# Another order of pieces and another map of the on-chip memory ahead of the first expert window

## The chip, the cores and the metric

The kernel runs on one core of one Trainium2 chip. The metric is the device time of one execution in microseconds (us); lower is better.

## What is computed

One inference step of a two-layer decoder trunk, all in fp32, for 512 prompt tokens and 8 new sample tokens (width 1024). Layer 0 mixes tokens with differential attention (8 heads; the sample tokens read a paged cache of keys and values), layer 1 with a short convolution. Each layer then runs PEER, a lookup of experts:

```
h = LN1(alpha*h + mixer(h))
h = LN2(alpha*h + PEER(h))
h = h + sigmoid(h @ Wg) * (p_i @ Wp)

PEER, per token: q = h @ w_q; scores of 8 heads against 2 x 128 keys; top 16 of each half,
top 16 of the 256 sums -> 16 expert ids and softmax gates g per head (128 experts a token)
a = <h, u_tab[id]>;  out = sum over experts of g * gelu(a) * v_tab[id]
```

Every token needs 128 rows of u and v (4 KB each) out of two tables of 16384 rows in each layer. The outputs are the rows h, the new keys and values of layer 0, and the convolution's state.

## The kernel before

**The engines' queues.** The program is written by hand for each engine. A planner (`Plan`) makes one list of "pieces" and every engine walks that list in its order and does its own part of each piece, so an engine that waits in one piece holds up all pieces behind it on that engine. TensorE makes products into four PSUM banks in turn, ScalarE (ACT) or VectorE (DVE) empties each bank, SyncE (SP) loads 1 MB panels of weights into two panel buffers, and GpSimd (POOL) issues the gathers of experts and the loads of cache pages.

**The lead.** First come 16 products of queries and keys. Then the list `lead` holds the attention: 32 units of scores (`score`), softmax on DVE and ACT (`weigh`), transposes (`turned`), and after each second unit of a head the sum over values (`summed`). Between them lie products that fill TensorE: value rows (`values[p][b]`, panel p and token tile b), key rows to be stored (`key_rows`), and the sample tokens' attention: `s_new`, `s_turn`, `s_probs`, `p_turn`, and the eight `s_out` products `out[k][half]`, each of which needs two samples' value pages. There is room for two samples' pages at a time, so POOL loads the next two when `out[k][1]` has read the last ones. `o_turn` transposes four samples' results. `square`, `ms0`/`ms1`, `root`, `factors` and `rms0`/`rms1` are the per-head normalization of the attention's output; group 0 is tiles 0 and 1, group 1 is tiles 2, 3 and the samples.

At the end of the lead the output projection is made for tile 0 (`m0`, four products, one for each panel of `mix`) and for tile 1 (`m1`), tile 0 is normalized (`a0`, `c0`) and transposed (`t0`), its query features are made (`q`) and its experts are chosen. Each head's choice is four pieces `r[4*hd:4*hd+4]`: key scores on TensorE, then some 10 us of DVE work; the fourth writes the ids that the gathers read, and the gates need an Exp on ACT. Line 1072 does that Exp in piece `route` with `x.i == 3`.

**The expert windows.** A window is one token tile: 128 experts in 64 pairs. For each expert POOL gathers 128 rows of 8 KB (1 MB, line 912) into one of 11 slots of the big on-chip buffer `arena`; DVE forms the dot product (line 1500), ACT the gelu and a diagonal matrix (line 1088), TensorE adds the rows into `acc` (line 1683), and that frees the slot. Background pieces (the next tiles' projections, features and choices) lie between the pairs: `early`, `rest`, `bg` in window 0. DVE and ACT run them two pairs late (`BEHIND = 2`), TensorE at their own place.

**The arena.** During the lead the same `arena` holds the attention's data, so a slot is free for its first gather only when these are dead. Before: slots 0 to 2 hold constants, logits and turned weights; slots 3 to 5 value rows and group 0's attention output; slots 6 to 8 the samples' values and the pages; slots 9 and 10 group 1's attention output, sample rows and factors. Gathers 0 to 5 wait for the ids alone, 6 to 8 for `out[3][1]` (line 909), 9 and 10 for the last `rms1` (line 911):

```
                    if e >= SLOTS_UV:
                        pool.wait_ge(slot_done, e - SLOTS_UV + 1)
                    elif e == HELD_BY_PAGES:
                        pool.wait_ge(bank_full, plan.sample_out[3][1].n + 1)
                    elif e == HELD_BY_SAMPLE:
                        read(pool, plan.last_rms)
```

**SP's queue.** `load_panel` goes through the panels in the order in which they were planned, and waits for the product that last read the buffer. The buffers take turns, but the first `pq` panel has a place of its own in `qT` ("queries"), which waits until all 16 `summed` are done. Ahead of the first `mix` panel (`keys_after`) SP waits for the last value product and loads the PEER keys, since `keys` holds the tokens of group 0 until then.

Of the kernel before, what the change touches and what calls it, by code (L numbers as in the profile page):

```python
# [57 lines left out]
HELD_BY_PAGES = 6  # L58
HELD_BY_SAMPLE = 9
# [60 lines left out]
class Plan:  # L120
# [31 lines left out]
    def settle(self):  # L152

        once = {("pq", 0, 0): "queries"}
# [23 lines left out]
    def lead(self):  # L178
# [4 lines left out]
        key_rows = [[product("k_rows", b=b, half=half) for half in range(2)] for b in range(BLOCKS)]  # L183
        values = [[product("v", self.v_panels[p], p=p, b=b) for b in range(BLOCKS)] for p in range(4)]
        values[0][0].fence = True
# [18 lines left out]
        for b in range(TB):  # L204
            if b >= 2:
                fill[b - 1].append(values[0][b])
            for half in range(2):
                fill[2 * b + half].append(key_rows[b][half])
# [7 lines left out]
        for k in range(4):  # L216
            fill[24 + k + 2 * (k // 2)].append(out[k // 2][k % 2])
        for k in range(2):
            fill[24 + k] += square[2 * k:2 * k + 2]

        lead = values[0][0:2] + key_rows[TB] + [Piece("s_new")]
# [139 lines left out]
    def build(self):  # L361
# [18 lines left out]
        def cut_at(pieces, share):  # L380
# [13 lines left out]
        self.keys_after = m0[0].panel  # L394
# [7 lines left out]
        self.last_rms = rms1[-1]  # L402
# [4 lines left out]
        lead += score[31] + [weigh[30], turned[29], ms0, roots[0], turned[30], f0, weigh[31], summed[6, 1]] + rms0[0] \  # L407
            + [turned[31], m0[0], summed[7, 1], m0[1], f1] + rms0[1] + [m1[0], o_turn[0], out[2][0], m1[1], out[2][1]] \
            + [m0[2], m0[3], a0, m1[2], m1[3], c0] + t0 + q[0:2] + r[0:1] + q[2:4] + r[1:3] + out[3] + [o_turn[1]] + r[3:7] \
            + [ms1, roots[1], f2] + rms1  # L410
        steps = [("alone", 0, 0, [lead])]
        early = r[7:8] + [a1, c1] + t1 + q[4:6] + late[0:2] + r[8:12] + late[2:4]
# [128 lines left out]
def build(nc, h0, h0T, consts, panels, ple_rows, keysT, uv0, uv1, cache_k, cache_v, pages, wlam, subg, ln, convw,  # L541
# [3 lines left out]
    with ctx:  # L545
# [61 lines left out]
        v_flat = part(TB * D)  # L607
        oT_early = part(C * G_W[0]).rearrange("p (c t) -> p c t", c=C)
        assert at[0] <= HELD_BY_PAGES * 2 * D
        at[0] = HELD_BY_PAGES * 2 * D  # L610

        v_new = part(D)
        kv_flat = part(4 * D)
        assert at[0] <= HELD_BY_SAMPLE * 2 * D
        at[0] = HELD_BY_SAMPLE * 2 * D

        oT_late = part(C * G_W[1])
        s_rows = part(D)
        rstd8 = part(G_W[0] + G_W[1])[0:HEADS, :]
        v_rows = [v_flat[:, b * D:(b + 1) * D] for b in range(TB)] + [v_new]  # L620
        oT = [oT_early, oT_late.rearrange("p (c t) -> p c t", c=C)]
        oT_normed = [oT[0], qT[:, q_off[1]:q_off[1] + C * G_W[1]].rearrange("p (c t) -> p c t", c=C)]
        kv_pages = kv_flat.rearrange("p (i j n) -> p i j n", i=2, j=2)


        q_all = oT_late[:, 0:2 * D].rearrange("p (i n) -> p i n", i=2)
# [7 lines left out]
        homes = {0: panel[:, 0, :], 1: panel[:, 1, :], "queries": qT[:, q_free:q_free + 2 * D]}  # L634
# [156 lines left out]
        def _(sp):  # L791
            sp.dma_start(h0T_early, h0T[:, :, 0:G_W[0]]).then_inc(s_hT, 16)

            def load_panel(i):
# [4 lines left out]
                elif home == "queries":  # L799
                    sp.wait_ge(a_o, len(SUMS))  # L800
                sp.dma_start(panel_of(i), panels[PANEL_AT[plan.panels[i]]]).then_inc(s_panel[home], 16)
# [58 lines left out]
        def _(pool):  # L860
# [34 lines left out]
            for b in range(BLOCKS):  # L895
                read(pool, plan.value_rows[b])
                dst = nv_p[b * P:(b + 1) * P, :] if b < TB else nv_s
                pool.dma_start(dst, v_rows[b][0:rows(b), :]).then_inc(v_out, 16)
# [960 lines left out]
```

## Time and profile before

| what | value |
|---|---|
| three runs | 3319.8, 3324.96, 3320.39 us (median 3320.39) |
| the profiled execution | 3319.8 us, of which 3317.9 us from its first to its last instruction |
| mean granted TensorE clock | 0.966 of full speed |
| TensorE, VectorE, ScalarE, GpSimd busy | 91%, 68%, 38%, 37% of the span |
| moved by DMA | 1248.09 MB, 376 GB/s over the span |

In the timeline each row is one or more like instructions: start and duration in us, engine, line, operation, result and operands, and in brackets the idle time of that engine just before and what ended it. PEld is TensorE's weight load. The windows give the busy time of each engine in a stretch, then the granted clock of TensorE (1.00 is 2.4 GHz, 0.50 is 1.2 GHz), the DMA engines' share and what they moved in GB/s.

### The profile page before, as it was taken

The page shows a single profiled execution, that of the slowest core. Times are in us where ns is not written, and L with a number is a line of the kernel's source. Part 1 is how long each engine was busy: PE and PEld are TensorE (multiplying, and loading weights), DVE is VectorE, ACT ScalarE, POOL GpSimd, SP SyncE. Part 2 cuts the span into 40 slices and gives each one's busy share as a digit, 9 for nine tenths or more (in the row PEclk, how much of TensorE's full clock was granted, in tenths as well). Part 3 has the DMA queues.
Part 4 walks back from the last instruction along what each step waited for, and adds up shares of the span by engine and source line. Part 5 has one row for each costly group of instructions (what it writes and reads, how often), then busy time and mean ns, then how long its engine had stood idle before and what let it go on. Part 6 is the DMA issues. An engine that isn't in the chain of part 4 may idle for free.

```text
span 3317.9 us, 33637 instructions
## 1 busy us (share of the span) xinstructions
PE 3011.4 (91%) x9426; PEld 1674.2 (50%) x9426; DVE 2251.0 (68%) x5801; ACT 1268.4 (38%) x3602; POOL 1232.5 (37%) x1100
## 2 busy tenths in 40 slices
PE   8998899989977899998898799999999788888887
PEld 7765555545533456554453355665455344443334
DVE  0653658787467867778768757764667888787454
ACT  0143334344233543333433464332434445435332
POOL 0100233443334333433443334444634435444441
PEclk9999799999999999999999899999999989999999
DMA  4513799999999999999899999999999999999997
GB/s 177 210 73 135 280 386 421 400 414 404 420 421 421 396 413 421 421 421 421 333 421 421 397 372 397 414 418 395 421 421 420 419 380 382 422 402 421 421 422 292
DMA packets 179818, 1248.09 MB, mean 376 GB/s; under 512 B 20086, under 2 KB 23414, under 8 KB 32432
## 3 DMA queue, kind: packets, MB, share of 16 engines
q0 software_dynamic: 156896, 1115.93, 82.3%
q1 hardware_dynamic: 22592, 128.97, 9.8%
q8 instruction: 75, 1.23, 0.1%
q10 hardware_dynamic: 144, 1.05, 0.1%
q14 instruction: 111, 0.91, 0.1%
HBM read 1239.41 MB, written 6.50 MB: 376 GB/s over the span
## 4 chain that ended last, share of the span: by engine, by line
PE 55%; DMA 18%; DVE 16%; ACT 4%; DVEq 4%; issue 3%; ACTq 1%; POOL 1%; POOLq 0%; SPq 0%
PE acc L1683 29%; DMA arena<-in_uv,idx 17%; PE bank L1709 10%; PE bank L1700 7%; DVE arena L1500 7%; PE bank L1538 3%; PE bank L1581 2%; DVEq L1408 2%; ACT diag L1088 1%; ACT L1072 1%; DVE ya L1343 1%; DVE ya L1354 1%; DVE h L1300 1%; DVE yb L1344 1%; DMA arena<-in_uv,small 1%
## 5 line engine op out<-in xcount | busy, mean ns | idle before, releaser
L1683 PE MATMUL acc<-arena,diag 128*128 128x512 f32 x4160 | 1940.1, 615 | 233.5 <-ACT diag L1088 233.1
L912 POOL DMA_INDIRECT arena<-in_uv,idx x1024 | 1185.3, 1158 | 1703.9 <-PE acc L1683 1594.9
L1500 DVE CUSTOM_DVE_ANT_0 arena<-arena,h 128x1024 f32<-128x1024 f32 x1024 | 1217.8, 1221 | 359.9 <-DMA arena<-in_uv,idx 356.8
L1683 PEld LDWEIGHTS acc<-arena,diag 128*128 128x128 f32 x4160 | 795.3, 196 | 1202.5 <-issue 833.2
L1078 ACT ACTIVATE act_w<-dots 128x2 f32<-128x2 f32 x520 | 105.5, 203 | 1433.3 <-DVE dots L1500 1432.7
L1088 ACT ACTIVATE diag<-cst,act_w 128x128 f32<-128x128 f32 x1040 | 368.6, 395 | 122.7 <-PE acc L1683 88.1
L1709 PE MATMUL bank<-hT,panel 128*128 128x264 f32 (+2 forms) x1792 | 403.7, 379 | 3.8 <-ACT hT L1045 3.8
L1709 PEld LDWEIGHTS bank<-hT,panel 128*128 128x128 f32 x1792 | 335.5, 190 | 99.4 <-issue 54.8
L1081 ACT ACTIVATE act_w<-act_w 128x1 f32<-128x1 f32 x1040 | 250.4, 287 | 43.7 <-issue 1.4
L1078 ACT ACT_TABLE_LOAD x128 | 164.2, 1283 | 1.6
L1700 PE MATMUL bank<-panel,hT 128*128 128x256 f32 (+1 forms) x576 | 131.8, 383 | 5.4 <-ACT hT L1045 5.4
L1700 PEld LDWEIGHTS bank<-panel,hT 128*128 128x128 f32 (+1 forms) x576 | 96.9, 170 | 49.3 <-issue 24.4
L1700 PE MATMUL bank<-panel,qT 128*128 128x256 f32 (+1 forms) x512 | 115.9, 379 | 0.0
L1700 PEld LDWEIGHTS bank<-panel,qT 128*128 128x128 f32 (+1 forms) x512 | 83.7, 165 | 40.1 <-issue 17.3
L1072 ACT ACT_TABLE_LOAD x80 | 102.6, 1283 | 1.4
L1337 DVE COPY yb<-tp 128x256 f32<-128x256 f32 x80 | 34.0, 425 | 94.8 <-PE tp L1667 89.6
L1415 DVE SCALAR_TENSOR_TENSOR h<-h,bank 128x256 f32<-128x256 f32 (+1 forms) x40 | 16.7, 419 | 109.0 <-PE bank L1700 107.8
L1500 DVE DVE_READ_ACCUMULATOR2_ANT dots<- 128x1 f32 x1040 | 85.0, 82 | 0.0
L1399 DVE RECIPROCAL ya<-ya 128x1 f32<-128x1 f32 x80 | 13.0, 163 | 83.2 <-ACT ya L1072 83.2
L1538 PE MATMUL bank<-keys,panel 128*128 128x256 f32 x256 | 60.8, 392 | 9.3 <-DMA panel<-in_panels 9.3
L1667 PEld LDWEIGHTS tp<-keys,qT 128*128 128x128 f32 (+1 forms) x320 | 43.3, 172 | 43.1 <-issue 42.1
L1382 DVE TENSOR_TENSOR yb<-ya,cst 128x512 f32<-128x512 f32 x80 | 55.4, 692 | 11.6 <-issue 0.6
(201 smaller groups left out, 2176.1 us busy)
## 6 DMA issues: line engine op xcount, KB each, us to landing
panel<-in_panels SPq DMA_DIRECT2D x103, 1024.0 KB
arena<-in_uv,idx POOLq DMA_INDIRECT x1024
arena<-in_cache_k POOLq DMA_DIRECT2D x16, 512.0 KB, 5.5
arena<-in_cache_v POOLq DMA_DIRECT2D x16, 512.0 KB, 5.0
arena<-out_y_s POOLq DMA_DIRECT2D x8, 512.0 KB, 6.0
arena<-in_panels SPq DMA_DIRECT2D x4, 1024.0 KB, 8.1
lng<-in_ln SPq DMA_DIRECT2D x6, 512.0 KB
lnb<-in_ln SPq DMA_DIRECT2D x6, 512.0 KB
```

The lines of the kernel that those rows point to most:

```text
L912: nc.gpsimd.indirect_dma_start(uv[:, e % SLOTS_UV, :], None, uv_dram[layer], bass.IndirectOffsetOnAxis(ids[:, r:r + 1], 0)).then_inc(gathe ...
L1072: nc.scalar.activation(r_ex, r_tv, ACT.Exp, bias=r_nm, accum_out=r_sum).then_inc(gexp_done, 1)
L1078: nc.scalar.activation(act_w[:, 1, half, s], dots[:, half, s], ACT.Gelu).then_inc(gelu_done, 1)
L1081: nc.scalar.activation(act_w[:, 2, half, r:r + 1], act_w[:, 1, half, r:r + 1], ACT.Copy, scale=act_w[:, 0, half, r:r + 1])
L1088: nc.scalar.activation(diag[:, r % DIAGS, :], mask, ACT.Copy, scale=act_w[:, 2, half, r:r + 1]).then_inc(diag_ready, 1)
L1408: dve.drain()
L1500: V.tensor_tensor_reduce(uv[:, e % SLOTS_UV, 0:D], uv[:, e % SLOTS_UV, 0:D], x_rows, 1.0, 0.0, ALU.mult, ALU.add, dots[:, G % 2, r:r + 1]) ...
L1538: m = mm(pj[n % 2][:, PW + G_OFF[g]:PW + G_OFF[g] + G_W[g]], w[:, c, :], src[g][:, c, 0:G_W[g]], start=(c == 0), stop=(c == C - 1))
L1581: t = mm(product_of[0:m, 0:PW], src[group_of(x.b)][:, c, local(x.b):local(x.b) + m], w[:, c, :], start=(c == 0), stop=(c == C - 1))
L1683: m = mm(acc[:, half * 512:(half + 1) * 512], diag[:, r % DIAGS, :], uv[:, e % SLOTS_UV, D + half * 512:D + (half + 1) * 512], start=False ...
L1700: last = mm(bank[0:m, x.n % BANKS, 0:PW], src[:, c, local(x.b):local(x.b) + m], weights[:, c, :], start=(c == 0), stop=(c == chunks - 1))
L1709: last = mm(bank[:, x.n % BANKS, 0:width], w[:, c, :], hT[:, c, lo:lo + width], start=(c == 0), stop=(c == C - 1))
```

## The change

The arena is mapped anew, pieces of the lead change places, and two of the `mix` panels get a buffer of their own.

- The arena: slots 3 and 4 hold group 1's attention output, sample rows and factors; slots 5 to 10 hold all value rows (the samples' too), group 0's output and the pages. The copies of the sample queries (`q_all`) move to the logits' place. Gathers 0 to 2 wait for the ids alone, 3 and 4 for the last `rms1`, and 5 to 10 for `last_mix`, tile 1's last projection product.
- Panels 2 and 3 of the first `mix` are loaded over the value rows, after all 16 sums are made and all value rows are stored; the PEER keys are loaded ahead of panel 2 instead of panel 0.
- Attention: the value products of tiles 0 and 1 move from the front of the lead into the first two units; the fence for the front goes to the key rows. The four `out` products go from units 24, 25, 28 and 29 to units 25 to 28, and the `square` pieces from 24 and 25 to 28 and 29.
- The end of the lead has a new order: `ms0` ahead of the last scores, tile 1's projection after its first product at the very end, `q[2:4]` and `o_turn[1]` behind the first head's whole choice, `out[3]` ahead of `q[0:2]` in part. The pieces `r[4:7]` go from the lead to the window. A Sqrt of one number ahead of the last squares goes.

```
@@
 FREE_AT_FIRST = 3
-HELD_BY_PAGES = 6
-HELD_BY_SAMPLE = 9
+FREE_NEXT = 5
@@ settle
-        once = {("pq", 0, 0): "queries"}
+        once = {("mix", 0, 2): "values0", ("mix", 0, 3): "values1", ("pq", 0, 0): "queries"}
@@ lead
+        key_rows[TB][0].fence = True
-        values[0][0].fence = True
         for b in range(TB):
-            if b >= 2:
-                fill[b - 1].append(values[0][b])
+            fill[b].append(values[0][b])
...
-            fill[24 + k + 2 * (k // 2)].append(out[k // 2][k % 2])
+            fill[25 + k].append(out[k // 2][k % 2])
-            fill[24 + k] += square[2 * k:2 * k + 2]
+            fill[28 + k] += square[2 * k:2 * k + 2]
-        lead = values[0][0:2] + key_rows[TB] + [Piece("s_new")]
+        lead = key_rows[TB] + [Piece("s_new")]
@@ build
-        self.keys_after = m0[0].panel
+        self.keys_after = m0[2].panel
-        lead += score[31] + [weigh[30], turned[29], ms0, roots[0], turned[30], f0, weigh[31], summed[6, 1]] + rms0[0] \
-            + [turned[31], m0[0], summed[7, 1], m0[1], f1] + rms0[1] + [m1[0], o_turn[0], out[2][0], m1[1], out[2][1]] \
-            + [m0[2], m0[3], a0, m1[2], m1[3], c0] + t0 + q[0:2] + r[0:1] + q[2:4] + r[1:3] + out[3] + [o_turn[1]] + r[3:7] \
-            + [ms1, roots[1], f2] + rms1
+        lead += [ms0] + score[31] + [weigh[30], turned[29], roots[0], f0, turned[30], weigh[31], summed[6, 1]] + rms0[0] \
+            + [turned[31], m0[0], summed[7, 1], m0[1], o_turn[0], out[2][0], m0[2], m0[3], f1, a0] \
+            + rms0[1] + [out[2][1], c0, m1[0]] + t0 + [out[3][0]] + q[0:2] + r[0:4] + [out[3][1], o_turn[1]] + q[2:4] \
+            + [ms1, roots[1], f2] + rms1 + m1[1:4]
-        early = r[7:8] + [a1, c1] + t1 + q[4:6] + late[0:2] + r[8:12] + late[2:4]
+        early = r[4:8] + [a1, c1] + t1 + q[4:6] + late[0:2] + r[8:12] + late[2:4]
@@ load_panel
-                elif home == "queries":
+                elif home in ("values0", "values1", "queries"):
                     sp.wait_ge(a_o, len(SUMS))
+                    sp.wait_ge(v_out, 16 * BLOCKS)
@@ gather_group
-                    elif e == HELD_BY_PAGES:
-                        pool.wait_ge(bank_full, plan.sample_out[3][1].n + 1)
-                    elif e == HELD_BY_SAMPLE:
+                    elif e == FREE_AT_FIRST:
                         read(pool, plan.last_rms)
+                    elif e == FREE_NEXT:
+                        pool.wait_ge(bank_full, plan.last_mix.n + 1)
@@ scalar, lead, ms0
-                    nc.scalar.activation(small[:, 61:62], eps, ACT.Sqrt)
```

## Rows read from the trace of the kernel before

**Rows 1.** The page: busy time, the gathers' queue, the gathers' group.

```profile
PE 3011.4 (91%) x9426; PEld 1674.2 (50%) x9426; DVE 2251.0 (68%) x5801; ACT 1268.4 (38%) x3602; POOL 1232.5 (37%) x1100
...
q0 software_dynamic: 156896, 1115.93, 82.3%
...
L912 POOL DMA_INDIRECT arena<-in_uv,idx x1024 | 1185.3, 1158 | 1703.9 <-PE acc L1683 1594.9
```

**Rows 2.** Windows: lead, first 56 us of the experts, and behind.

```profile
0.00:384.00 384.00, 348.88 (x1609) 255.37 (x1610) 163.20 (x474) 94.63 (x259) 38.76 (x67) 0.94 0.44 162
384.00:440.00 56.00, 50.58 (x182) 28.85 (x180) 37.95 (x88) 22.86 (x66) 24.77 (x20) 0.94 0.90 335
440.00:880.00 440.00, 418.93 (x1274) 231.99 (x1275) 319.44 (x831) 171.93 (x514) 179.03 (x159) 0.97 1.00 411
880.00:1400.00 520.00, 466.37 (x1357) 251.68 (x1356) 380.61 (x990) 206.46 (x597) 207.98 (x190) 0.98 1.01 416
```

**Rows 3.** Timeline where the attention begins.

```profile
127.24 7.14 PE L1581 MATMUL bank<-panel,keys 128*128 128x256 f32 x32 [0.89 <-ACT qT L956]
...
134.86 1.28 DVE L1254 COPY x_sample<-bank 8x512 f32<-8x512 f32 x2 [1.70 <-PE bank L1573]
...
139.89 0.70 PE L1586 MATMUL bank<-qT 64*128 64x256 f32 x2 [3.00 <-DVE small L1220]
```

**Rows 4.** Timeline: the second and third sample products and the pages between.

```profile
252.36 1.91 PE L1629 MATMUL bank<-arena,x_sample 128*32 128x512 f32 x8
...
255.57 0.55 POOL L875 DMA_DIRECT2D arena<-in_cache_v  x1 [10.21 <-issue]
...
264.43 3.44 PE L1629 MATMUL bank<-arena,x_sample 128*32 128x512 f32 x8 [2.13 <-DMA arena<-in_cache_v]
```

**Rows 5.** The critical chain, a page load (0.5 MB).

```profile
259.08 5.22 DMA arena<-in_cache_v
```

**Rows 6.** Timeline: Sqrt's table, tile 0's and tile 1's projection, panels.

```profile
281.61 1.28 ACT L1020 ACT_TABLE_LOAD   x1
...
292.28 3.69 PE L1700 MATMUL bank<-panel,arena 128*128 128x256 f32 x16 [0.56 <-DVE arena L1273]
...
305.57 5.14 PE L1700 MATMUL bank<-panel,arena 128*128 128x256 f32 x16 [1.15 <-DVE arena L1273]
...
310.74 9.51 SPq L801 DMA_DIRECT2D panel<-in_panels  x2
...
322.64 14.08 PE L1700 MATMUL bank<-panel,arena 128*128 128x256 f32 x64
```

**Rows 7.** Timeline: first head's choice and the first nine gathers (first, ninth).

```profile
348.03 0.68 PE L1667 MATMUL tp<-keys,qT 128*128 128x128 f32 x4 [0.57 <-ACT qT L1053]
...
348.75 0.42 DVE L1337 COPY yb<-tp 128x256 f32<-128x256 f32 x1 [9.95 <-PE tp L1667]
...
358.35 0.17 DVE L1393 SCALAR_TENSOR_TENSOR idx<-ya 128x16 int32<-128x16 f32 x1
...
359.40 1.00 POOL L912 DMA_INDIRECT arena<-in_uv,idx  x1 [32.41 <-DVE idx L1393]
...
369.42 0.93 POOL L912 DMA_INDIRECT arena<-in_uv,idx  x1 [0.30 <-issue]
```

**Rows 8.** Timeline: the end of the lead.

```profile
374.42 7.38 PE L1654 MATMUL bank<-arena,cst 8*128 8x264 f32 x16 [3.70 <-DVE arena L1245]
...
382.52 1.23 DVE L1500 CUSTOM_DVE_ANT_0 arena<-arena,h 128x1024 f32<-128x1024 f32 x1 [0.20 <-issue]
382.59 1.97 POOL L912 DMA_INDIRECT arena<-in_uv,idx  x1 [12.24 <-DVE qT L1419]
```

**Rows 9.** Timeline: the 32nd gather's issue, and two dots that wait.

```profile
451.81 0.93 POOL L912 DMA_INDIRECT arena<-in_uv,idx  x1 [3.34 <-PE acc L1683]
...
457.52 1.23 DVE L1500 CUSTOM_DVE_ANT_0 arena<-arena,h 128x1024 f32<-128x1024 f32 x1 [1.24 <-DMA arena<-in_uv,idx]
460.00 1.22 DVE L1500 CUSTOM_DVE_ANT_0 arena<-arena,h 128x1024 f32<-128x1024 f32 x1 [1.25 <-DMA arena<-in_uv,idx]
```

More of the change, by code:

```diff
@@ L401, in build @@
         rms1 = [self.product(Piece("rms1", hd=hd)) for hd in range(HEADS)]
-        self.last_rms = rms1[-1]
+        self.last_mix, self.last_rms = m1[3], rms1[-1]
         self.ms0, self.ms1 = ms0, ms1
@@ L605, in build @@
         at[0] = FREE_AT_FIRST * 2 * D
[L607 to L617, printed above, removed]
+        oT_late = part(C * G_W[1]).rearrange("p (c t) -> p c t", c=C)
         s_rows = part(D)
         rstd8 = part(G_W[0] + G_W[1])[0:HEADS, :]
-        v_rows = [v_flat[:, b * D:(b + 1) * D] for b in range(TB)] + [v_new]
-        oT = [oT_early, oT_late.rearrange("p (c t) -> p c t", c=C)]
+        assert at[0] <= FREE_NEXT * 2 * D
+        at[0] = FREE_NEXT * 2 * D
+        v_flat = part(BLOCKS * D)
+        v_rows = v_flat.rearrange("p (b n) -> p b n", b=BLOCKS)
+        oT = [part(C * G_W[0]).rearrange("p (c t) -> p c t", c=C), oT_late]
         oT_normed = [oT[0], qT[:, q_off[1]:q_off[1] + C * G_W[1]].rearrange("p (c t) -> p c t", c=C)]
+        kv_flat = part(4 * D)
         kv_pages = kv_flat.rearrange("p (i j n) -> p i j n", i=2, j=2)
-        q_all = oT_late[:, 0:2 * D].rearrange("p (i n) -> p i n", i=2)
+        q_all = logit_flat[:, 0:2 * D].rearrange("p (i n) -> p i n", i=2)
         wl = wT_flat[:, 0:4 * HD]
@@ L633, in build @@
         q_free = q_off[1] + C * G_W[1]
-        homes = {0: panel[:, 0, :], 1: panel[:, 1, :], "queries": qT[:, q_free:q_free + 2 * D]}
+        homes = {0: panel[:, 0, :], 1: panel[:, 1, :], "values0": v_flat[:, 0:2 * D], "values1": v_flat[:, 2 * D:4 * D], "queries": qT[:, q_free:q_free + 2 * D]}
         k_new = x_sample
@@ L897, in _ @@
                 dst = nv_p[b * P:(b + 1) * P, :] if b < TB else nv_s
-                pool.dma_start(dst, v_rows[b][0:rows(b), :]).then_inc(v_out, 16)
+                pool.dma_start(dst, v_rows[0:rows(b), b, :]).then_inc(v_out, 16)
             for i in range(NS + 2, 2 * NS):
@@ L977, in lead @@
                     m = rows(x.b)
-                    nc.scalar.activation(v_rows[x.b][0:m, x.p * PW:(x.p + 1) * PW], product_of[0:m, 0:PW],
+                    nc.scalar.activation(v_rows[0:m, x.b, x.p * PW:(x.p + 1) * PW], product_of[0:m, 0:PW],
                                          ACT.Copy).then_inc(bank_free[x.n % BANKS], 1)
@@ L1571, in lead @@
                     m = rows(x.b)
+                    if x.fence:
+                        all_read(pe, len(ORDER))
                     for k in range(4):
@@ L1577, in lead @@
                     m, w = rows(x.b), panel_of(x.panel).rearrange("p (c n) -> p c n", c=C)
-                    if x.fence:
-                        all_read(pe, len(ORDER))
                     for c in range(C):
@@ L1604, in lead @@
                         lo = P if kb == blocks - 1 else 0
-                        t = mm(acc[:, at + lo:at + 2 * P], v_rows[kb][:, hd * P:(hd + 1) * P], wT[g][:, kb, lo:2 * P],
+                        t = mm(acc[:, at + lo:at + 2 * P], v_rows[:, kb, hd * P:(hd + 1) * P], wT[g][:, kb, lo:2 * P],
                                start=(kb == 0), stop=(kb == blocks - 1), skip_group_check=True)
@@ L1633, in lead @@
                     for b in two:
-                        m = mm(product_of[b % 4 * 32:b % 4 * 32 + 32, :], s_weight_new[0:NS, b, :], v_new[0:NS, cols],
+                        m = mm(product_of[b % 4 * 32:b % 4 * 32 + 32, :], s_weight_new[0:NS, b, :], v_rows[0:NS, TB, cols],
                                start=False, stop=True)
```

## The prediction, made before the changed kernel ran

> **What bounds the kernel now.** I read the page first: TensorE is busy 91% of the span, but the gathers' queue alone takes 82.3% of the time of all 16 DMA engines, and POOL spends most of its idle time waiting for TensorE to free a slot [rows 1]. The windows then split the run in three [rows 2]. From 440 us on the DMA engines are full (share 1.00 or 1.01, 411 to 416 GB/s). Before 384 us they move 162 GB/s: the lead is bound by TensorE and by the chains between engines. In the 56 us between, DMA runs at 335 GB/s. The pitch at which landed gathers let the dots go is 2.48 us [rows 9], so one gather of 1.05 MB moves at some 423 GB/s, the most that is seen. Two things follow. The end comes when 1040 gathers have gone through a full queue, so whatever moves the filling of that queue moves the end by as much. And the first 56 us hold 56 x (1 - 335/423) = 11.6 us in which DMA could have done more: a store of slack for a DMA queue that starts late, but only if slots are free.
>
> **Step 1, the start of the attention.** Before, TensorE fills the time until DVE is free for the first key rows with two value products (7.14 us, at 127.24), and later waits 3.00 us for the first scores [rows 3]. Now key rows and scores come first, two banks of four need DVE, and DVE is busy until about 133.6 us with the sample queries (it took the key rows at 134.86 after 1.70 us of idle time behind its coefficients [rows 3]). I make TensorE stand from 129 to 133.9 us, 4.9 us in place of 3.0: +2 us. Bounds: 0 (some later wait takes it up) and +3.6 (a whole value product, half of the 7.14). TensorE has hardly a gap in the following 100 us, so I carry it.
>
> **Step 2, the pages in the attention.** From the start of the product that reads the pages last to the landing of the next two samples' pages it takes 264.43 - 252.36 = 12.1 us; POOL's first issue is 3.2 us after that start and the last page needs 5.22 us [rows 4, 5]. Before, three units lay between; now one does. The work between shrinks by some 3 us, partly bought back because the first two products come a unit later, so the wait of 2.13 us [rows 4] grows to about 4.3: +2.2 us, bounds 0 and +5. Putting `ms0` ahead of the last scores lets the first four heads' sums go without a wait, but ACT now loads Sqrt's table (1.28 us, [rows 6]) between the last weights' copy and the root, where `f0`, `rms0` and `m0[0]` queue behind it: +0.6, bounds -2 and +3. The Trainium skill ("ScalarE: Activation LUTs", What ACT_TABLE_LOAD costs) has 1.28 us too, and adds 1.38 us of drain for each switch of tables; with that drain on this path the term would be +2.0 and the total 1.4 us more.
>
> **Step 3, to the first expert ids.** From `m0[0]` (292.28) to the first key scores (348.03) it takes 55.8 us [rows 6, 7]. Three of tile 1's four products leave this stretch; four projection products in a row take 14.08 us [rows 6], so 3 x 3.52 = -10.6. One half of `out[3]` comes in: +3.0 (its matmuls like those of [rows 4], 1.91 us, and the new rows' part). `out[3]` needs pages that POOL can only ask for when `out[2][1]` has read the last ones; 12.1 us later they are there, while only `m1[0]` (3.6), the wait for the norm and two transposes lie between: about 4 us of TensorE's wait that was no wait before. Gone are the wait and half-speed product at 305.57 (5.14 us in place of 3.5 [rows 6]), the 2 us in which `t0` waited for the norm behind `m1[3]`, and the gap behind the second factor: -7 together. Sum -10.6; bounds -14 and -4. The panels 2 and 3 now wait for the last sum, but so does nothing else: `m0[1]`, `o_turn[0]` and `out[2][0]` are 8.6 us of work, and SP's two panels were not waited for either when they were asked at 310.74 and needed from 322.64 [rows 6]. So the first ids come 2 + 2.2 + 0.6 - 10.6 = -5.8 us, about 352.6 in place of 358.35, and the first gather starts at about 353.6 in place of 359.40 [rows 7].
>
> **Step 4, from the first ids to the window.** Before, nine gathers go out one behind the other by 369.42 [rows 7]; the tenth waits for the last `rms1`, until 382.59, and the first dot starts at 382.52 [rows 8]. Now three go out at once, two more after the last `rms1`, and the six others after `m1[3]`. From the key scores (348.03) to the end of the `rms1` products (374.42 + 7.38 = 381.8) it takes 33.8 us [rows 7, 8]. Added: `m1[1:4]` 10.6; and ACT's Exp for the first head's gates, which stood behind `o_turn[1]`, now stands ahead of the copy of `out[3][1]` that `o_turn[1]` reads. The choice of a head takes 9.8 us on DVE (348.75 to 358.52), the maximum that the Exp needs comes after about 6 of them [rows 7], plus 1.28 for the table: TensorE waits some 6 us ahead of `o_turn[1]` where it waited 0.9: +5.1. Gone: `out[3][0]` (-3.0), the second head's key scores and DVE's share of its choice ahead of `f2` (-2.4). Sum 44.1 in place of 33.8, +10.3; bounds +7 and +15. So TensorE is through with the lead 10.3 - 5.8 = +4.5 us later, and the sixth gather starts at about 387 us.
>
> **Step 5, in the window.** Three pieces of the second head's choice (`r[4:7]`) now run on DVE between the fourth and the fifth dot, ahead of `a1` and `c1`, for whose result the next thing in TensorE's queue, tile 1's transposes, waits; all gathers from the 16th on wait for slots that are freed behind that. Price: the first three of four pieces took from 348.75 to about 356, 7.2 us [rows 7]. Consumer chain: 4.5 + 7.2 = +11.7. I cost it in full, since nothing is free there; before, these 7.2 us lay under `ms1` and the root.
>
> **Sum.** The 32nd gather was issued at 451.81 and its dot started at 460.00 [rows 9]: 8.2 us, where a gather that meets an empty queue needs about 5 (the page's 5.22 for half the bytes, [rows 5]; the nine first ones spread over their time). So 3.2 us of the 11.7 are taken up by queueing, and the DMA engines are late by 8.5 from there on, when they are full [rows 2]. The other chain is the DMA queue by itself: four gathers fewer are in when the window begins (4 x 2.48 = 9.9) and it starts 4.5 later, 14.4, less at most 11.6 of slack: +2.8. The larger decides: +8.5. The profiled execution took 3319.8, 0.6 below the median of 3320.39. **I predict 3328.5 us.**
>
> **Rivals.** (a) *The slack takes up the consumers' delay*: DVE finds the choice's pieces while it waits anyway, and the DMA chain alone decides: +2.8, or 0 if the lead is 3 us shorter than I have it: 3320 to 3324. For it: the ring is emptier, so DVE waits for gathers in any case. Against: the fifth dot came only after work, not after a landing, and slots 5 to 10 are asked for in time for it. Chance 0.23. (b) *Faster*: the new order removes more waits in the lead than it adds. TensorE stands for 384 - 348.9 = 35 us of the lead, at a mean clock of 0.94 [rows 2], so there is something to win. If the Exp doesn't hold `o_turn[1]` (-5.1), the pages are in time (-6.2) and step 1 is free (-2), the lead ends at -8.8 and the end at -5 to -8; it decides from -11 at the window's start: 3313. For it: ten us fewer work ahead of the ids. Against: each of these waits is a queue order that can be read in the code. Chance 0.13. (c) *A longer lead*: panels 2 and 3 come too late for `m0[2]`, since both, the norm's parameters and the queries' panel now queue at once behind the last sum (4 MB, 10 us at the pitch of [rows 9]), and the longer waits leave TensorE at half speed for the products behind them (5.14 for 3.5 in [rows 6]): +4 and +4, 3337. Chance 0.12. The Trainium skill ("TensorE: Matmul & The Clock Gate", What's actually happening) says that the engine's clock is halved after idleness and is given back by work; the half-speed product behind a wait agrees. (d) *The forecast*, carried delay, +4 to +14: 0.52.
>
> **Numbers.** A measurement of this kernel can tell about 0.2%, 6.6 us, from no change. Slower by more: 0.42 of (d), all of (c), 0.03 of (a), together 0.57. Within: 0.10 of (d), 0.20 of (a), 0.01 of (b), together 0.31. Faster: the rest of (b), 0.12. Range: with the bounds of steps 1 to 4 the forecast runs from 3319 to 3338; a few us beyond on both sides leave out 2 in 10: 3316 to 3341.
>
> **What the profile after would show.** The first ids at 351 to 354 and the third gather at once, then a gap in the gathers until some 376, six in a row from 387. A wait of TensorE of 5 to 6 us ahead of `o_turn[1]` ended by ACT, one of about 4 ahead of `out[3][0]` ended by a page. `c1` at about 410 in place of 398. DMA at 440 us full again. I am wrong if the window begins before 383, if the DMA engines move more than before from 384 to 440 us, or if the end's shift differs from the shift of the first full stretch, which would mean that the delay is taken up later.

## The result and the profile after

The changed kernel takes 3346.42 us (median of four runs, 3342.72 to 3351.05) against 3320.80 us before in the same comparison. The ratio is 1.0076, 95% interval 1.0058 to 1.0093: 25.6 us slower. The direction was forecast, the forecast size was a third of it (8.5 us), and the time lies 5 us beyond the range. Medians here and below leave out three executions that took far longer than the others of their kernel (3397.8 and 7911.1 us of the kernel before, 9423.8 us of a_all).

The profiled execution has a span of 3341.6 us, 23.7 more than before. The page of the changed kernel, the same lines as [rows 1]:

```profile
PE 3011.3 (90%) x9426; PEld 1674.9 (50%) x9426; DVE 2249.6 (67%) x5801; ACT 1269.3 (38%) x3601; POOL 1226.2 (37%) x1100
...
q0 software_dynamic: 156896, 1115.93, 81.7%
```

Work and bytes are the same, so the 23.7 us are time in which nobody does more. The windows of the changed kernel, cut at its own start of the expert windows (397 us in place of 381.7), answer to [rows 2]:

```profile
0.00:397.00 397.00, 351.37 (x1601) 255.32 (x1602) 154.66 (x439) 94.86 (x258) 33.77 (x62) 0.92 0.40 146
397.00:453.00 56.00, 43.53 (x145) 25.08 (x144) 35.14 (x93) 18.26 (x54) 21.58 (x19) 0.85 0.85 322
453.00:880.00 427.00, 404.22 (x1239) 222.64 (x1238) 320.26 (x844) 169.35 (x500) 177.71 (x154) 0.97 1.00 410
880.00:1400.00 520.00, 464.85 (x1357) 252.17 (x1356) 372.16 (x954) 206.68 (x595) 208.84 (x190) 0.98 1.01 415
```

What changes is in the first two: 15.6 us more until TensorE begins the first window, a lower granted clock (0.92 for 0.94, then 0.85 for 0.94), and in the first 56 us behind it TensorE busy 43.5 in place of 50.6 us. ([rows 2] starts this stretch 2.3 us behind its window's start; counted from that start, 381.73, the kernel before has 52.0 us busy at a clock of 0.92.) From there on the rates are those of before.

**Step 1, start of the attention.** Timeline of the changed kernel:

```profile
126.67 1.03 PE L1568 MATMUL bank<-cst,qT 128*8 128x128 f32 x8 [0.89 <-ACT qT L950]
...
133.53 5.20 PE L1574 MATMUL bank<-panel,keys 128*128 128x256 f32 x16 [5.40 <-DVE x_sample L1247]
```

TensorE waits 5.40 us for DVE's key rows, as forecast (4.9). But the 3.00 us wait for the scores [rows 3] is gone, the third unit's scores start at 143.78 in place of 146.35 us, and the work behind closes up: the last value product of the samples starts at 240.83 in place of 240.53 us, so the step costs 0.3 us, not 2. (TensorE reached this place 0.6 us earlier, 126.67 for 127.24; counted from there it is 0.9.)

**Step 2, the pages in the attention.** Timeline, answering to [rows 4]:

```profile
256.08 1.91 PE L1622 MATMUL bank<-arena,x_sample 128*32 128x512 f32 x8
...
259.29 0.55 POOL L869 DMA_DIRECT2D arena<-in_cache_v  x1 [13.63 <-issue]
...
268.10 3.62 PE L1622 MATMUL bank<-arena,x_sample 128*32 128x512 f32 x8 [6.72 <-DMA arena<-in_cache_v]
271.66 1.92 PE L1627 MATMUL bank<-arena,x_sample 8*32 8x512 f32 x4
273.50 0.69 PE L1587 MATMUL tp<-cst,arena 128*128 128x128 f32 x2
274.12 1.65 PE L1579 MATMUL bank<-qT 64*128 64x384 f32 x4
275.70 3.63 PE L1622 MATMUL bank<-arena,x_sample 128*32 128x512 f32 x8
```

From the second product to the landing it is 12.0 us, as before. The wait is 6.72 us (forecast 4.3, before 2.13), and the row says a second thing: the same eight matmuls that took 1.91 us take 3.62 behind the wait, and the next pair of sample products again 3.63. From the product at 268.10 to the end of the second pair it is some 5.6 us more than these products take at full speed. That second slow pair is not there in every execution: in a_exp and a_early, below, whose order is the same up to there, the first pair takes 3.63 behind its wait and the second 1.91. Then the table load for the root, with `ms0`, the sum of squares, now ahead of the last scores:

```profile
293.05 1.13 PE L1579 MATMUL bank<-qT 64*128 64x512 f32 x4
...
297.25 0.58 ACT L988 ACTIVATE arena<-tp 128x512 f32<-128x512 f32 x1
297.84 1.28 ACT L961 ACT_TABLE_LOAD   x1
299.14 0.47 ACT L961 ACTIVATE arena<-bank,small 8x256 f32<-8x256 f32 x1
...
304.03 5.29 PE L1693 MATMUL bank<-panel,arena 128*128 128x256 f32 x16 [0.56 <-DVE arena L1266]
```

The first projection product (292.28 in [rows 6]) starts at 304.03, 11.8 us later, and it too runs slowly (5.29 for 3.69). The table load costs 1.30 us from end to end; the 1.38 us of drain that the Trainium skill adds to it ("ScalarE: Activation LUTs", What ACT_TABLE_LOAD costs) don't show on this path, so there the measurement decides.

**Steps 3 and 4, to the ids and to the window.**

```profile
346.19 1.91 PE L1622 MATMUL bank<-arena,x_sample 128*32 128x512 f32 x8 [1.66 <-DMA arena<-in_cache_v]
...
354.35 0.68 PE L1660 MATMUL tp<-keys,qT 128*128 128x128 f32 x4 [0.57 <-ACT qT L1046]
...
362.31 3.54 PE L1632 MATMUL bank<-cst,arena 128*128 128x4 f32 x16 [4.46 <-issue]
...
366.17 1.00 POOL L906 DMA_INDIRECT arena<-in_uv,idx  x1 [25.07 <-DVE idx L1386]
...
385.52 0.94 POOL L906 DMA_INDIRECT arena<-in_uv,idx  x1 [15.84 <-DVE qT L1412]
...
397.34 1.88 PE L1668 MATMUL acc<-h,cst 128*128 128x512 f32 x4
397.77 0.94 POOL L906 DMA_INDIRECT arena<-in_uv,idx  x1 [10.07 <-PE bank L1693]
```

The first key scores come at 354.35, 6.3 us later than in [rows 7] and not 5.8 earlier. The gathers come as forecast in kind, three, two and then six, each group late: the sixth starts at 397.77.

**Step 5, the first window.** The chain that ended last, then gather 32 and its dot, answering to [rows 9]:

```profile
402.92 0.42 DVE yb L1330
...
417.93 1.28 DVE h L1283
...
420.96 1.09 PE bank L1724 x4
```

```profile
477.29 0.94 POOL L906 DMA_INDIRECT arena<-in_uv,idx  x1 [3.33 <-PE acc L1676]
```

```profile
485.77 1.23 DVE L1493 CUSTOM_DVE_ANT_0 arena<-arena,h 128x1024 f32<-128x1024 f32 x1 [1.24 <-DMA arena<-in_uv,idx]
```

DVE takes the second head's choice at 402.92, and TensorE's transposes of tile 1 start at 420.96, 23.6 us behind the window's start in place of 16.6 (398.33 less 381.73). The 32nd gather is issued 25.5 us late, and its dot starts 25.8 us late, 8.5 us behind the issue as before (8.2). Nothing was taken up. Seven of the us that the window adds lie ahead of the transposes (23.6 for 16.6). The other 2.8 lie behind them: TensorE has waited 10.27 us there in place of 2.90, and the transposes and the eight expert products behind take 1.09 and 6.03 us in place of 0.63 and 3.60. The changed kernel, then the kernel before:

```profile
420.96 1.09 PE L1724 MATMUL bank<-cst,h 128*128 128x128 f32 x4 [10.27 <-DVE h L1293]
421.84 6.03 PE L1676 MATMUL acc<-arena,diag 128*128 128x512 f32 x8
```

```profile
398.33 0.63 PE L1731 MATMUL bank<-cst,h 128*128 128x128 f32 x4 [2.90 <-DVE h L1300]
398.79 3.60 PE L1683 MATMUL acc<-arena,diag 128*128 128x512 f32 x8
```

### The profile page after: what moved, and what is told of

It is laid out like the page before. It is cut to its first block, busy times and chain, and to the rows that moved or that the text cites. A ratio compares the mean times of both kernels' runs of the same rounds, so it can differ in the third digit from the quotient of the medians.

```text
span 3341.6 us, 33639 instructions
## 1 busy us (share of the span) xinstructions
PE 3011.3 (90%) x9426; PEld 1674.9 (50%) x9426; DVE 2249.6 (67%) x5801; ACT 1269.3 (38%) x3601; POOL 1226.2 (37%) x1100
## 4 chain that ended last, share of the span: by engine, by line
PE 54%; DMA 17%; DVE 17%; ACT 4%; DVEq 4%; issue 3%; POOL 1%; ACTq 1%; POOLq 0%; SPq 0%
PE acc L1676 29%; DMA arena<-in_uv,idx 15%; PE bank L1702 10%; PE bank L1693 7%; DVE arena L1493 7%; PE bank L1574 2%; DVEq L1401 2%; PE bank L1531 2%; ACT diag L1081 1%; ACT L1065 1%; POOL arena L906 1%; DMA arena<-out_y_s 1%; DVE ya L1336 1%; PE bank L1579 1%; DVE yb L1337 1%
## 6 DMA issues: line engine op xcount, KB each, us to landing
lnb<-in_ln SPq DMA_DIRECT2D x6, 512.0 KB, 15.6
```

## The experiments

Theory A: each us that the chain up to tile 1's transposes gets longer is carried to the end, and the change's 25 us are the sum of such pieces. Rival B: the new map of the arena, which lets only three gathers out early, is the cost. Times are medians, each with the kernel before on the same chip; the difference is to that one, and the ratio is of the same two sets. For the changed kernel it is +25.6 us.

| run | edit | us (before) | difference | ratio, 95% interval | gather 32 issued | span less that |
|---|---|---|---|---|---|---|
| before | | | | | 451.8 | 2866.1 |
| after | the change | 3346.4 (3320.8) | +25.6 | 1.0076, 1.0058 to 1.0093 | 477.3 | 2864.3 |
| b_window | before, r[4:7] in the window | 3328.1 (3321.7) | +6.4 | 1.0019, 1.0007 to 1.0030 | 459.1 | 2865.0 |
| b_hold | before, gathers 3 to 10 late | 3324.8 (3321.7) | +3.1 | 1.0007, 0.9997 to 1.0016 | 455.9 | 2863.5 |
| b_carry | before, 10 us of matmuls | 3326.7 (3321.2) | +5.5 | 1.0010, 1.0000 to 1.0020 | 463.7 | 2866.1 |
| a_attn | after, sample products back | 3336.2 (3321.7) | +14.5 | 1.0040, 1.0026 to 1.0054 | 468.7 | 2867.4 |
| a_early | after, r[4:7] back | 3342.2 (3321.7) | +20.5 | 1.0056, 1.0038 to 1.0074 | 473.9 | 2866.3 |
| a_exp | after, Exp's piece later | 3337.4 (3321.7) | +15.7 | 1.0048, 1.0031 to 1.0065 | 470.3 | 2864.1 |
| a_ms0 | after, ms0 and Sqrt back | 3344.6 (3321.7) | +22.9 | 1.0069, 1.0052 to 1.0085 | 479.7 | 2864.2 |
| a_warm | after, one wait filled | 3342.0 (3321.7) | +20.3 | 1.0062, 1.0045 to 1.0078 | 474.5 | 2864.4 |
| a_fill | after, five waits filled | 3336.4 (3321.5) | +14.9 | 1.0047, 1.0033 to 1.0061 | 468.8 | 2865.9 |
| a_all | after, all four moves undone | 3324.8 (3321.7) | +3.2 | 1.0016, 1.0006 to 1.0026 | 463.0 | 2859.7 |
| b_out | before, sample products earlier | 3316.6 (3321.2) | -4.6 | 0.9986, 0.9977 to 0.9995 | 452.0 | 2866.6 |
| b_fill | b_out, two waits filled | 3311.9 (3321.2) | -9.4 | 0.9977, 0.9965 to 0.9989 | 441.5 | 2862.5 |

Two versions are compared with each other through these differences, and that is coarse: half the interval's width is 3 to 6 us for each, so a difference between two of them is good to some 7 or 8 us. Against the changed kernel the intervals of a_attn and a_all are clear, those of a_exp and a_fill overlap at their edge, and those of a_early, a_warm and a_ms0 overlap widely; for these the traces have to carry the reading.

The last two columns are of each kernel's one profiled execution. The last is the strongest single finding: whatever was done ahead of it, the time from the 32nd gather to the end is 2860 to 2867 us, while the gather itself moves by 38 us. So a few rows at 450 us into the run tell the time at 3320, to some 4 us. The largest exception is a_all: its gather 32 is 11.2 us late and its span only 4.8, so that 6.4 us were taken up behind gather 32, and no run shows where. Tile 1's transposes, the place that theory A names, tell it as well: over the twelve experiments and the change their shift runs from -10 to +25 us, and that of the span differs from it by 4.8 us at most.

**b_window**, the window's part alone.

```
-            + [m0[2], ..., c0] + t0 + q[0:2] + r[0:1] + q[2:4] + r[1:3] + out[3] + [o_turn[1]] + r[3:7] \
+            + [m0[2], ..., c0] + t0 + q[0:2] + r[0:1] + q[2:4] + r[1:3] + out[3] + [o_turn[1]] + r[3:4] \
-        early = r[7:8] + [a1, c1] + ...
+        early = r[4:8] + [a1, c1] + ...
```

> The kernel before with one edit: the second head's pieces r[4:7] go from the lead to the first window. Theory A (each us that the path from tile 1's norm to TensorE's transposes gets longer is carried to the end whole): DVE's 7.0 us ahead of tile 1's norm, some 2 us of TensorE at half speed behind that wait, less about 1 us of a shorter lead: +7 to +9 us over before, and all gathers from the 17th on shifted by the same. Rival B (the delay of the changed kernel comes from the new map of the arena, which lets only 3 gathers out early): 0 to +2 us here.

Measured +6.4 us (the interval of the ratio makes it 2 to 10), a little under A's 7 to 9; gather 32 +7.3. Tile 1's norm ends at 403.8 in the timeline of its DVE, against 398.2 before, although the lead was 1.4 us shorter:

```profile
402.52 1.28 DVE L1300 SCALAR_TENSOR_TENSOR h<-h,rstd,lnb 128x1024 f32<-128x1024 f32 x1
```

Theory A holds; B's 0 to 2 does not.

**b_hold**, the ring's part alone.

```
-                    elif e == HELD_BY_PAGES:
-                        pool.wait_ge(bank_full, plan.sample_out[3][1].n + 1)
-                    elif e == HELD_BY_SAMPLE:
+                    elif e == FREE_AT_FIRST:
                         read(pool, plan.last_rms)
```

> The kernel before, with gathers 3 to 10 all held until the last rms1, nothing else: the ring is filled as late as in the changed kernel against the start of its window. Theory A: the DMA engines have time to catch up while TensorE and DVE are busy with tile 1's norm and queries: +1 to +4 us over before. Rival B: most of the 25 us of the change: +12 or more.

Measured +3.1 us, not told from zero; gather 32 is 4.1 us late in the profiled execution and the span 1.5. Eight gathers go out later, the sixth by 20 us, and the end hardly moves: B is refuted as the main cause.

**a_attn** and **a_early**, the change with one part undone.

```
-            fill[25 + k].append(out[k // 2][k % 2])
+            fill[24 + k + 2 * (k // 2)].append(out[k // 2][k % 2])
-            fill[28 + k] += square[2 * k:2 * k + 2]
+            fill[24 + k] += square[2 * k:2 * k + 2]
```

> The changed kernel with the four sample products and the squares back at their old units (24, 25, 28, 29 and 24, 25), nothing else. Theory A: the wait for pages falls from 6.7 to some 2 us and the half-speed products behind it go: 4 to 8 us faster than the changed kernel, the first projection product of tile 0 earlier by as much. Rival B: no difference (within 2 us).

11.1 us less than the change, more than expected. The wait falls to 4.26 us only, where some 2 was expected, and the product behind it still takes 3.63, but the first projection product starts at 297.93 in place of 304.03, and the window at 388.9 in place of 397.3:

```profile
266.41 3.63 PE L1622 MATMUL bank<-arena,x_sample 128*32 128x512 f32 x8 [4.26 <-DMA arena<-in_cache_v]
```

Gather 32 comes 8.6 us earlier. The edit moves the sample products and the squares at once, so how much belongs to either was not tried.

```
-            ... + [out[3][1], o_turn[1]] + q[2:4] \
+            ... + [out[3][1], o_turn[1]] + q[2:4] + r[4:7] \
             + [ms1, roots[1], f2] + rms1 + m1[1:4]
...
-        early = r[4:8] + ...
+        early = r[7:8] + ...
```

> The changed kernel with r[4:7] back in the lead (behind q[2:4]), nothing else; DVE has 10.5 us of idle time there before the factors. Theory A: 7 to 10 us faster than the changed kernel, the start of the window unchanged to 1 us and tile 1's norm 7 us earlier behind it. Rival B: no difference (within 2 us).

5.1 us less, gather 32 3.4 us earlier: below the 7 to 10 expected, and by the times alone not told from nothing. The window's start was not unchanged but 3.7 us later (401.02). The timeline of TensorE shows why: the first `rms1` now waits 5.37 us for DVE (2.50 in the changed kernel's wait at the same place), which is still at the second head when the root is ready. So the idle time that I counted on was partly too early:

```profile
372.14 3.73 PE L1550 MATMUL bank<-hT,cst 128*8 128x264 f32 x16
381.24 7.37 PE L1647 MATMUL bank<-arena,cst 8*128 8x264 f32 x16 [5.37 <-DVE arena L1238]
```

**a_exp**, the Exp's place.

```
-            ... + r[0:4] + [out[3][1], o_turn[1]] + q[2:4] \
+            ... + r[0:3] + [out[3][1], o_turn[1]] + r[3:4] + q[2:4] \
```

> The changed kernel with one piece moved: the first head's fourth piece (the one with ACT's Exp) goes behind out[3][1] and o_turn[1]. Theory A (a wait on the lead's path is carried whole): TensorE's 4.5 us wait ahead of o_turn[1] and its half speed behind go, 4 to 7 us faster than the changed kernel. Rival C (the squares of ms1 wait for the same Exp, which now stands directly ahead of them, so that the wait only moves): 0 to 2 us.

9.9 us less, more than expected. From the first key scores (354.08) to the window's start (390.36) it is 36.3 in place of 43.0 us: 6.7 of the 9.9 are at the place of the edit. Rival C's 0 to 2 does not hold there. The wait ahead of `o_turn[1]` is 0.85 us and its matmuls take 1.92 in place of 3.54:

```profile
358.43 1.92 PE L1632 MATMUL bank<-cst,arena 128*128 128x4 f32 x16 [0.85 <-issue]
```

**a_ms0**, the order around the last scores.

```
-        lead += [ms0] + score[31] + [weigh[30], turned[29], roots[0], f0, turned[30], ...
+        lead += score[31] + [weigh[30], turned[29], ms0, roots[0], turned[30], f0, ...
...
                 elif x.kind == "ms0":
+                    nc.scalar.activation(small[:, 61:62], eps, ACT.Sqrt)
                     act.drain()
```

> The changed kernel with ms0 behind the last scores again and the early Sqrt of one number back, nothing else. Theory A: the last scores come 4 us earlier and the table load leaves the path of the first factors; 2 to 6 us faster than the changed kernel. Rival D (the order here is neutral, as the prediction had it at +0.6): within 1.5 us.

2.7 us less, but the intervals of the two ratios overlap nearly whole, and in its profiled execution the lead was 2.4 us longer. Inconclusive; the term is small either way.

**a_warm** and **a_fill**, the clock by itself.

```
                     pe.wait_ge(s_weighted, 1)
...
+                    if x.part == 1 and x.half == 0:
+                        for _ in range(7):
+                            mm(product_of[:, 0:512], const("ident"), cst[:, 0:512], start=True, stop=True)
                     for b in two:
                         pe.wait_ge(s_pair[b % 2], 32 * ((NS + b) // 2 + 1))
```

> The changed kernel with seven matmuls of constants (128x512, some 6 us) put ahead of the wait for pages in the third sample product; their result is overwritten. The wait stays, but TensorE works in it. Theory E (most of the 7 us by which this part cost more than forecast is half speed behind the wait): the four sample products behind run at 1.9 in place of 2.8 to 3.6 us, and the first projection product starts 3 to 6 us earlier; 3 to 6 us faster. Rival F (the wait alone is the loss): no gain, up to 1 us slower.

5.3 us less, with intervals that overlap. The work is the same and more, the page lands no earlier, and the sample products behind it run at full speed:

```profile
265.27 6.28 PE L1620 MATMUL bank<-cst 128*128 128x512 f32 x14
271.95 1.91 PE L1625 MATMUL bank<-arena,x_sample 128*32 128x512 f32 x8 [0.40 <-DMA arena<-in_cache_v]
...
275.99 1.91 PE L1625 MATMUL bank<-arena,x_sample 128*32 128x512 f32 x8
```

From the first sample product to the first projection product it is 47.9 us in place of 51.8. (That execution was 3.7 us late ahead of the edit already, which is why the projection product itself starts at 303.81; the lead varies by some 4 us from one execution to the next.) Of that gain only a part is sure: with nothing filled and the same order, this stretch took 51.9 us in a_early and 48.5 in a_exp, where the second pair ran at full speed anyway. So a_warm shows what filling a wait does to the products right behind it; how much it gains, one execution can't tell.

a_fill has such matmuls in five waits:

> The changed kernel with matmuls of constants in five waits of the lead (seven ahead of the third sample product, two ahead of the seventh, five ahead of o_turn[1], two ahead of tile 1's rms0, three ahead of the first rms1); their results are never read. Every wait stays; only TensorE's clock can differ. Theory E (half speed behind waits is a third or more of the change's cost): 8 to 12 us faster than the changed kernel, the window's start at 386 to 390 in place of 397. Rival F: within 5 us of it (the one filled wait gave 4.5).

10.7 us less, and the window starts at 389.2. The granted clock between 240 and 400 us is 0.93 in place of 0.83 (before: 0.85). First the changed kernel, then a_fill:

```profile
240.00:400.00 160.00, 130.92 (x551) 78.81 (x550) 53.36 (x165) 40.24 (x104) 14.22 (x21) 0.83 0.36 129
```

```profile
240.00:400.00 160.00, 140.05 (x606) 81.43 (x605) 60.64 (x194) 43.39 (x114) 20.39 (x27) 0.93 0.41 148
```

One part of this does not depend on the spread from one execution to the next. From the first key scores to the window, where two of the five waits are filled, it takes 36.8 us; the four kernels with the same order and nothing filled there (the changed kernel, a_attn, a_ms0, a_warm) have 43.0, 42.7, 42.9 and 42.8. (The two matmuls ahead of the seventh sample product did not help: 5.07 us of wait are left behind them, and that product takes 3.59 us.) These 6 us are nearly all that a_exp won there by taking the wait away (36.3). So theory E holds: some 6 us in this part by the traces and 10.7 in all by the medians, where only the clock can differ. F's 5 us are not excluded by the medians alone. This is the whole gain of five fillings in the changed kernel, not the change's share; the kernel before has such waits too.

**a_all**, the four moves undone together.

> The changed kernel with all four moves undone (sample products and squares, ms0 and the early Sqrt, the Exp's piece, r[4:7] in the lead); the new map of the arena, the gathers' holds, the two panels over the value rows and tile 1's projection at the end stay. Theory A: what is left is tile 1's projection at the end of the lead and the later ring, which cost next to nothing as long as the first ids come earlier: within 5 us of the kernel before (3317 to 3327). Rival B (the map and the late gathers): still 10 us or more above it.

+3.2 us over before by the medians, so 22.4 of the change's 25.6 us go; the ratio of 1.0016 makes it +5.3 (2 to 9). That is what stays: the map, the holds, the two panels' places and tile 1's projection at the end. A's forecast was 3317 to 3327, and 3324.8 lies in it; B's 10 us or more is outside the interval.

**b_carry**, a known delay at the window's start.

```
                 elif x.kind == "rms1":
                     pe.wait_ge(rstd_ready, 3)
+                    if x.hd == 0:
+                        for _ in range(12):
+                            mm(product_of[:, 0:512], const("ident"), cst[:, 0:512], start=True, stop=True)
```

> The kernel before with twelve matmuls of constants (128x512, 10.3 us) ahead of the first rms1 product; their result is overwritten. Nothing else in order, map or holds. Theory A (a delay of the whole consumer side at the window's start goes to the end whole): 7 to 10 us slower than before (10.3 less what the work behind gains at full speed), and gather 32 and the end shifted alike. Rival G (the prediction's view that the queue of gathers takes up some 3 us, or more): 7 us or less at the end, less there than at the window's start.

+5.5 us in the median (0 to 6.6 by the interval), below A's 7 to 10; the edit lengthens its own place by 7.4 us (key scores to window 41.1 in place of 33.7). The profiled execution is another 4.6 us late ahead of the edit, and there gather 32 and the span are both 11.8 us above before, to 0.1 us. So the carrying is whole in that execution, and in the median neither A nor G is decided: 5.5 for 7.4 would be a quarter taken up, but it is not told from the whole.

**b_out** and **b_fill**, versions that the above points to.

```
-            fill[24 + k + 2 * (k // 2)].append(out[k // 2][k % 2])
+            fill[23 + k + 3 * (k // 2)].append(out[k // 2][k % 2])
```

> The kernel before with the first two sample products one unit earlier (23 and 24 in place of 24 and 25), so that four units lie between them and the third. Theory A: the 2.1 us wait for pages and the half speed behind it go: 2 to 5 us faster than before. Rival: within 1.5 us, because the softmax chain of those units is what TensorE waits for then.

4.6 us faster than before (0.9986, 0.9977 to 0.9995): the wait for pages is 0.57 us, the product behind it takes 1.91. The profiled execution doesn't show the gain at its end: it has the first projection product 3.4 us earlier (288.86), then 6.62 us for tile 1's first, and gather 32 as before.

```
                 elif x.kind == "rms0":
+                    if x.b == 1 and x.half == 0:
+                        for _ in range(2):
+                            mm(product_of[:, 0:512], const("ident"), cst[:, 0:512], start=True, stop=True)
                     pe.wait_ge(rstd_ready, x.b + 1)
...
                 elif x.kind == "rms1":
+                    if x.hd == 0:
+                        for _ in range(4):
+                            mm(product_of[:, 0:512], const("ident"), cst[:, 0:512], start=True, stop=True)
                     pe.wait_ge(rstd_ready, 3)
```

> The one before (b_out) with matmuls of constants in two waits of the lead: two ahead of tile 1's first rms0 and four ahead of the first rms1; their results are overwritten. Theory E (half speed behind waits costs): tile 1's first projection product takes 3.7 in place of 5.1 us and the first window's start 1.9 in place of 3.8; 1 to 4 us faster than b_out. Rival: no difference from b_out, since DVE sets the pace behind both.

9.4 us faster than before, 0.9977 (0.9965 to 0.9989), the fastest of all; its interval overlaps b_out's. Tile 1's first projection product takes 3.69 us where it took 5.14 in [rows 6], and from the first key scores to the window it is 28.4 us in place of 33.7 (b_hold 32.4, b_out 32.6):

```profile
297.42 1.88 PE L1649 MATMUL bank<-cst 128*128 128x512 f32 x4
299.23 2.05 PE L1652 MATMUL bank<-arena,cst 8*128 8x128 f32 x16
302.42 3.69 PE L1706 MATMUL bank<-panel,arena 128*128 128x256 f32 x16 [1.15 <-DVE arena L1273]
```

## Why the prediction was off by a factor of three

| step | forecast | measured in the profiled execution |
|---|---|---|
| 1, start of the attention | +2 | +0.3 |
| 2, pages, ms0, table load | +2.8 | +11.5 (304.03 - 292.28 - 0.3) |
| 3, to the first key scores | -10.6 | -5.4 (50.3 in place of 55.75) |
| 4, to the window's start | +10.3 | +9.3 (43.0 in place of 33.7) |
| 5, DVE's pieces in the window | +7.2 | +7.0 to tile 1's transposes, +2.8 behind |
| taken up by the queue | -3.2 | 0 |
| at gather 32 | +8.5 | +25.5 |

*Step 4 and DVE's share of step 5* were right in mechanism: the Exp ahead of a copy that TensorE waits for, and three pieces of DVE's work ahead of the norm. Runs a_exp and b_window show both apart. Step 5's size was right (7.0 for 7.2), but the 2.8 us behind the transposes had no term at all: they are slow products behind a wait, as in step 2. That step 4's sum came out within 1 us is in part luck. The wait ahead of `o_turn[1]` grew by 3.6 us (4.46 for 0.89) and not 5.1; tile 1's three products took 12.7 (384.66 to 397.34) and not 10.6, since the first ran at 5.94; and from the start of `ms1`'s products to the end of `rms1`'s it was 12.8 in place of 17.6 us.

*Step 2 failed by size, by 8.7 us.* The page wait was put at 4.3 us and was 6.7: between the end of the second product and the wait lay 2.4 us of work, where I had taken some 5. The larger miss is that I priced the work behind the wait at full speed. The rows before showed it (3.44 us for the product behind the 2.13 us wait [rows 4], 5.14 behind 1.15 [rows 6]) and I named it in rival (c), but only for four us. Runs a_attn, a_warm and a_fill show it. Part of the 8.7 belongs to the one execution: from the last value product to the first projection product it is 63.2 us here and 63.4 in a_early, but 59.9 in a_exp, with the same order up to there, which leaves a miss of 5.4. The rule that I cited, an engine halved by idleness (the Trainium skill, "TensorE: Matmul & The Clock Gate", What's actually happening), agrees with them; what was missing is that each new wait of several us has two prices, its own length and the slow work behind it.

*Step 3 failed by size, by 5.2 us.* I had the half-speed products of this stretch vanish with their waits. They did not: tile 0's first product takes 5.29 us, its third and fourth 8.64 together where four take 14.08 [rows 6], and tile 1's first 5.08. The wait for the last pages was 1.66 us and not 4. Other runs show that the two replace each other: where the products right ahead of the pages ran at full speed that wait was 3.58 us (a_warm), 6.67 (a_ms0) and 5.07 behind 1.88 us of constants (a_fill), with a product of 3.6 in place of 1.91 behind it, and the stretch still took 47.9, 49.4 and 51.3 us, against the 45.2 that I forecast.

*The last step failed in kind.* I let the queue of gathers take up 3.2 us of the delay, since a gather waited in it for that long. But that queue is made of gathers issued as TensorE frees slots, the delayed engine itself, so it comes later with it and is as long as before (8.5 us from issue to dot in place of 8.2). The tables above show that nothing was taken up; the reason is my reading of the queue, and b_carry, made to test it, was not decided in its median. As I read it, a queue takes up a delay only of somebody who doesn't fill it. The second chain, DMA alone, for which I had +2.8, was the right one to apply to the holds: b_hold measures +3.1.

*The range* was narrower than its terms. All upper bounds of steps 1 to 4 together are 18.1 us above the forecast, 3346.6, and I took 3341, as if misses of different steps were independent. Step 3 (-5.4) stayed within its own bounds; step 2 with +11.5 passed its +8 (the 8.2 of a_exp's execution pass it by little). Both missed upward for one reason. The total itself has a slip: 8.5 on 3319.8 or on 3320.39 gives 3328.3 or 3328.9, not 3328.5; nothing hangs on it.

The rivals: (a), DVE waits anyway, is excluded by the 25.5 us; (b), faster, too; (c), a longer lead, is nearest, but its first mechanism is not seen: the panels over the value rows are asked for at 310.86 and TensorE takes them at 321.32 without a wait. The forecast (d) had the mechanism and not the size. Of what the profile was to show, the gap between the third and the fourth gather, the six in a row and the full DMA behind came; the times of all of them were some 10 us off. The wait ahead of `o_turn[1]` was 4.46 us and not 5 to 6. None of the three signs of being wrong came: the window begins at 397, the DMA engines move 319 GB/s from 384 to 440 us (335 before), and the end's shift, 23.7, is that of gather 32 to 1.8 us. They tested the mechanism, and none of them the size.

One thing is open: the four undone parts give 11.1, 5.1, 9.9 and 2.7 us apart, 29 in sum, and 22.4 together (20.3 by the ratios). Each of the parts is uncertain by some 7 us, so this is no contradiction, and how much is overlap was not tried.

## What to carry to other kernels

Where one stretch is a chain through several engines and the stretch behind it is full, price every new wait in the chain twice: its length, and the TensorE work behind it at half speed. Don't count slack in a queue that the delayed engine feeds. And look for one event soon behind the change (here the 32nd gather) whose shift is that of the end, here to some 4 us and once to 6: it tells variants apart in one execution where the times need many.

## What the runs showed of the hardware beyond that

A wait of TensorE of 1.15 us stood ahead of tile 1's first projection product, and that product took 5.14 us in the kernel before and 6.62 in b_out, where b_fill's, with constants ahead of the wait before, took 3.69; behind the 1.66 us wait at 346.19 the changed kernel's product ran at its full 1.91. So a short wait is at times followed by slow products and at times not. The lead's length varies by some 4 us between executions of kernels that are alike up to there (first key scores at 352.61 us in b_carry, 348.03 before), and in b_carry that went to the end whole; that it makes most of the spread of the times is likely but not shown. Matmuls of constants in a wait (6.3 us of them in a 6.7 us wait) keep the clock up (0.93 in place of 0.83 from 240 to 400 us in a_fill) and cost nothing that the runs show as long as they end with the wait; the medians of a_fill and b_fill are 10.7 and 4.8 us below those of the kernels without them, the second within overlapping intervals.
